# Split-product attention for two heads at a time, run between the projection tiles of the other heads

## The reference

```python
q, k, v, f_logit, c_b, c_c, c_in, gate_a, gate_c = split_cols(u @ w_in)
log_f = log_sigmoid(f_logit + b_forget)
F = cumsum(log_f, axis=1)
s = einsum('bqhd,bkhd->bhqk', q, k) * 64 ** -0.5
s = s + F_q[..., None] - F_k[:, :, None, :]
s = where(k_pos <= q_pos, s, -inf)
y_attn = einsum('bhqk,bkhd->bqhd', softmax(s), v)
y_conv = c_b * short_conv(c_c * c_in, conv_w)
mixed = (sigmoid(gate_a) * (y_attn @ w_attn_branch) + sigmoid(gate_c) * (y_conv @ w_conv_branch)) @ w_out
```

## Time and profile before

| | |
|---|---|
| median of 3 runs | 2390.04 us |
| the profiled execution, as a run | 2395.49 us |
| its span | 2393.8 us |
| TensorE busy | 2243.4 us, 94% |
| VectorE busy | 1019.3 us, 43% |
| ScalarE busy | 712.7 us, 30% |
| POOL busy | 620.3 us, 26% |
| granted TensorE clock, mean | 0.91 |

### The profile page before, as it was taken

How to read it: one execution, slowest core, us unless ns; L and a number is a source line. 1 busy time by engine, 2 the same in 40 slices (tenths; PEclk the granted TensorE clock), 3 DMA queues, 4 the chain that set the end, 5 groups by cost and what they waited for, 6 DMA issues and landing times.

```text
span 2393.8 us, 29247 instructions
## 1 busy us (share of the span) xinstructions
PE 2243.4 (94%) x11946; PEld 1857.1 (78%) x11946; DVE 1019.3 (43%) x1621; ACT 712.7 (30%) x909; POOL 620.3 (26%) x147
## 2 busy tenths in 40 slices
PE   6999985999997999979999997999999988999997
PEld 6698874888766666669999997887578776888886
DVE  4699764423327566542322235302442324332224
ACT  2422232322225545431111123323342223122121
POOL 0334300234310000024433331231004332434430
PEclk6999985799998999989999996898569997999998
DMA  8455400132214999732222221121003321232210
GB/s 245 135 179 183 137 18 1 36 106 88 70 36 141 337 341 342 279 106 89 88 90 92 98 88 36 54 88 54 0 1 107 105 71 53 89 104 88 94 64 36
DMA packets 176219, 261.30 MB, mean 109 GB/s; under 512 B 13209, under 2 KB 141898, under 8 KB 176126
## 3 DMA queue, kind: packets, MB, share of 16 engines
q1 hardware_dynamic: 175550, 258.96, 32.2%
q10 hardware_dynamic: 576, 1.05, 0.1%
HBM read 257.88 MB, written 2.11 MB: 109 GB/s over the span
## 4 chain that ended last, share of the span: by engine, by line
PE 82%; DVE 14%; issue 1%; ACT 1%; DMA 1%; SPq 0%; DVEq 0%; ACTq 0%
PE PS L690 56%; PE PS L1109 6%; PE PS L1131 4%; PE PS L924 3%; DVE macc L1760 2%; PE PS L1223 2%; PE PS L746 1%; DVE Hf L1731 1%; DVE sc L1875 1%; DVE max L1874 1%; PE PS L915 1%; DVE macc L1758 1%; DVE Hf L1712 1%; PE PS L890 1%; PE PS L840 1%
## 5 line engine op out<-in xcount | busy, mean ns | idle before, releaser
L652 POOL TENSOR_TENSOR w_lo<-w_raw,w_hi 128x2048 fp32r<-128x2048 f32 x133 | 617.9, 4648 | 1689.6 <-ACT w_hi L1313 1689.6
L690 PE MATMUL PS<-HH,w_hi 128*128 128x512 f32 (+1 forms) x1936 | 598.2, 347 | 25.2 <-DVE HL L1705 25.2
L690 PE MATMUL PS<-HL,w_hi 128*128 128x512 f32 (+1 forms) x1936 | 598.7, 347 | 0.0
L690 PE MATMUL PS<-HH,w_lo 128*128 128x512 f32 (+1 forms) x1936 | 596.3, 346 | 0.0
L1313 ACT ACTIVATE w_hi<-w_raw 128x2048 fp32r<-128x2048 f32 x133 | 254.3, 1913 | 534.0 <-PE PS L690 491.9
L690 PEld LDWEIGHTS PS<-HH,w_hi 128*128 128x128 f32 x1936 | 339.2, 191 | 74.8 <-issue 28.0
L690 PEld LDWEIGHTS PS<-HL,w_hi 128*128 128x128 f32 x1936 | 338.5, 190 | 45.5
L690 PEld LDWEIGHTS PS<-HH,w_lo 128*128 128x128 f32 x1936 | 338.1, 190 | 45.0
L2278 DVE TENSOR_TENSOR actf<-PS,sg 128x528 f32<-128x528 f32 (+1 forms) x44 | 30.8, 700 | 421.0 <-PE PS L690 421.0
L2289 DVE TENSOR_TENSOR yacc<-yacc,PS 128x528 f32<-128x528 f32 (+1 forms) x176 | 122.4, 695 | 105.7 <-PE PS L690 105.7
L2171 DVE TENSOR_TENSOR m_lo<-m_raw,m_hi 128x2048 fp32r<-128x2048 f32 x56 | 128.1, 2292 | 77.3 <-ACT m_hi L1520 76.8
(11 more groups left out here) (356 smaller groups left out, 2878.8 us busy)
## 6 DMA issues: line engine op xcount, KB each, us to landing
w_raw<-in_w_in SPq DMA_DIRECT2D x49, 1024.0 KB, 5.1
w_raw<-in_w_ffn_in SPq DMA_DIRECT2D x44, 1024.0 KB, 4.9
m_raw<-in_w_exp_gate SPq DMA_DIRECT2D x56, 512.0 KB, 4.3
m_raw<-in_w_exp_up SPq DMA_DIRECT2D x56, 512.0 KB, 5.5
m_raw<-in_w_exp_down SPq DMA_DIRECT2D x56, 512.0 KB, 4.8
w_raw<-in_w_ffn_out SPq DMA_DIRECT2D x22, 1024.0 KB, 4.8
mod_raw<-in_w_mod SPq DMA_DIRECT2D x20, 1024.0 KB, 5.0
w_raw<-in_w_out SPq DMA_DIRECT2D x8, 1024.0 KB, 5.0
```

Source lines behind the costliest of these rows:

```text
L652: pool.tensor_tensor(w_lo[:, s, :], w_raw[:, s, :], w_hi[:, s, :].bitcast(F32), ALU.subtract).then_inc(split, 1)
L690: ins = mm(o, l, r, **k)
```

## The change

1. The ring of weights has two arrays instead of three: `w_lo` lies where `w_raw` lies. So the load of chunk c waits for TensorE's start of chunk c−2 (`begun`), not for the split of c−3. The slot of expert chunk 3 moves to the freed room at the other end.
2. The spread of the forget sums is gone. VectorE writes the sums' hi and lo parts to `FS` and a selecting matrix `selF`, and a fourth product adds them to the logits; a fifth, of the identity and the mask `outR`, adds the mask.
3. Q, K, V and the probabilities are split into hi (ScalarE) and lo (VectorE), and logits and values are made of three products each. A step handles two heads (partitions 0 to 63 and 64 to 127) and one query tile; the values of two query tiles are made at once. There are 16 steps.
4. The chunks of `P2` come in the order K, Q, V of heads 0 to 3, then K, Q, V of heads 4 to 7. Behind each of the 9 tiles of the latter one attention step (`fox_step`) is issued; the others follow after.

```diff
-        w_raw = at("w_raw", B, [RING, CH]); B += RING * CH * 4
+        w_raw = at("w_raw", B, [RING, CH])
+        w_lo = at("w_lo", B, [RING, CH], F32R); B += RING * CH * 4
         w_hi = at("w_hi", B, [RING, CH], F32R); B += RING * CH * 4
-        w_lo = at("w_lo", B, [RING, CH], F32R); B += RING * CH * 4
...
-        for x, off in enumerate([BASE + 16384 * q for q in range(4)] + [A0 + 49152, A0 + 16384]):
+        for x, off in enumerate([BASE + 16384 * q for q in range(3)] + [A0 + 81920, A0 + 49152, A0 + 16384]):
...
-              ("fm", K2), ("fm", K2 + 256), ("fm", Q2), ("fm", Q2 + 256), ("tm", V2), ("tm", V2 + 256)]
-        FORGET_AT, SPREAD_AT = 2, 4
+              ("fm", K2), ("fm", Q2), ("tm", V2), ("fm", K2 + 256), ("fm", Q2 + 256), ("tm", V2 + 256)]
+        KQV = [c0 for _, c0 in P2[6:]]
+        FOX_FROM = 9
+        FORGET_AT = 2
+        FOX = [(m, i) for m in range(4) for i in range(NTOK)]
...
                 if c >= RING:
-                    sp.wait_ge(split, c - RING + 1 + more)
+                    sp.wait_ge(begun, c - RING + 2 + more)
...
+            def fox_logits(m, i):
...
+                cols = [slice(0, min(512, n_all))] + ([slice(512, n_all)] if n_all > 512 else [])
+                for n, (q_, k_) in enumerate(((qh, kh), (qh, kl), (ql, kh), (None, None))):
+                    for cs in cols:
+                        for e in range(2):
+                            hp = slice(64 * e, 64 * e + 64)
+                            if n < 3:
+                                mm(outs[e][:, cs], q_[hp, m, rows], k_[hp, m, cs], start=n == 0, stop=False, skip_group_check=True)
+                            else:
+                                h = 2 * m + e
+                                mm(outs[e][:, cs], selF[hp, h:h + 1].to_broadcast([64, P]), FS[hp, cs], start=False, stop=False,
+                                   skip_group_check=True)
+                d0 = META + P * i
...
+                        ins = mm(outs[e][:, c0:cs.stop], identR[:, :], outR[:, c0 - d0:cs.stop - d0], start=False, stop=True,
+                                 skip_group_check=True)
...
+            def fox_transposes(x):
...
+                pe.wait_ge(pn2_ready, x + 1)
+                for part in range(1 if i < NTOK - 1 else 2):
...
+                            nc.tensor.transpose(PS[:, s, b, P * j:P * j + P], src[:, META + P * j:META + P * j + P], ident[:, :])
...
+            def fox_values(x):
...
+                W.wait_released(tgroup[x])
+                s = W.claim()
+                for e in range(2):
...
+                    for j in [4] + list(range(2 * hf_ + 2)):
+                        q0 = P if j == 2 * hf_ + 1 else 0
...
+                        for n, (l, r) in enumerate(((vh, ph_), (vl, ph_), (vh, pl_))):
+                            ins = mm(o[:, q0:256], l[kp, j, vs], r, start=j == 4 and n == 0, stop=j == 2 * hf_ + 1 and n == 2,
+                                     skip_group_check=True)
...
+            def fox_step():
+                n = at_step["n"]
+                at_step["n"] += 1
+                if n == 8:
+                    for g in range(1, 5):
+                        W.wait_released(W.g - g)
+                if n < len(FOX):
+                    fox_logits(*FOX[n])
+                if 0 <= n - 2 < len(FOX):
+                    fox_transposes(n - 2)
+                if 0 <= n - 4 < len(FOX) and FOX[n - 4][1] % 2 == 1:
+                    fox_values(n - 4)
...
-                if n_p == SPREAD_AT:
+                after = None
+                if n_p >= FOX_FROM:
+                    after = fox_step
...
+            while at_step["n"] < len(FOX) + 4:
+                fox_step()
```

More of the change, by code:

```diff
@@ L718, in fm_chunk @@
                     W.made(ins)
+                    if after is not None:
+                        after()
                 cur["h"] = None
@@ L722, in h_operands, with tm_chunk @@
                 return (lambda k: HH[:, k, t0_:t0_ + T]), (lambda k: HL[:, k, t0_:t0_ + T])
-            def tm_chunk(tiles):
+            def tm_chunk(tiles, after=None):
                 s_w = begin_chunk()
@@ new lines, in fox_transposes @@
+            def fox_transposes(x):
+                m, i = FOX[x]
+                pe.wait_ge(pn2_ready, x + 1)
+                for part in range(1 if i < NTOK - 1 else 2):
+                    s = W.claim()
+                    for e in range(2) if i < NTOK - 1 else (part,):
+                        src = pr2[:, x % 3, e, :]
+                        for j in range(i + 1):
+                            b = e if i < NTOK - 1 else 0
+                            nc.tensor.transpose(PS[:, s, b, P * j:P * j + P], src[:, META + P * j:META + P * j + P], ident[:, :])
+                        b, c0 = (e, P * (i + 1)) if i < NTOK - 1 else (1, 0)
+                        ins = nc.tensor.transpose(PS[0:META, s, b, c0:c0 + P], src[:, 0:META], ident[:, :])
+                    W.made(ins)
+                tgroup[x] = W.g - 1
@@ new lines, in _ @@
+            for x, c0 in enumerate(KQV):
+                next_hi()
+                for t in range(2 if x % 3 < 2 else 5):
+                    s = W.arrive()
+                    W.skip(1)
+                    m = 2 * (x // 3) + t
+                    if x % 3 == 0:
+                        ins = af(sv(kh[:, m, :], TALL), ps(s, TALL), ACT.Copy)
+                    elif x % 3 == 1:
+                        ins = af(qh[:, m, :], ps(s), ACT.Copy)
+                    else:
+                        n, vc = P if t < 4 else META, c0 - V2
+                        ins = af(vh[0:n, t, vc:vc + 256], PS[0:n, s, 0, 0:256], ACT.Copy)
+                    ins.then_inc(kqv_hi, 1)
+                    if x >= 3:
+                        fox_step()
@@ L2326, in _ @@
             W.skip(1)
+            L.mark(ts(FS[:, :], ones[:, 0:1].to_broadcast([P, TALL]), 0.0, None, ALU.mult))
+            L.mark(ts(selF[:, :], ones[:, 0:8], 0.0, None, ALU.mult))
+            L.mark(v_.tensor_copy(identR[:, :], ident[:, :]))
+            L.mark(v_.tensor_copy(outR[:, :], outside[:, :]))
+            L.wait()
+            for b in range(4):
+                L.mark(v_.tensor_copy(selF[32 * b:32 * b + 8, :], ident[32 * b:32 * b + 8, 32 * b:32 * b + 8]))
             dve.wait_ge(gla_act, 2 + seq + 1 + 1)
@@ new lines, in _, with fox_step @@
+            t_at = {}
+            at_step = {"n": 0}
+            def fox_step():
+                n = at_step["n"]
+                at_step["n"] += 1
+                if 0 <= n - 3 < len(FOX):
+                    fox_lo(n - 3, t_at[n - 3])
+                if n < len(FOX):
+                    fox_max(n)
+                if 0 <= n - 1 < len(FOX):
+                    fox_scale(n - 1)
+                if 0 <= n - 2 < len(FOX):
+                    t_at[n - 2] = W.g
+                    W.skip(1 if FOX[n - 2][1] < NTOK - 1 else 2)
+                if 0 <= n - 4 < len(FOX) and FOX[n - 4][1] % 2 == 1:
+                    W.skip(1)
```

252 lines of the change are left out of this document (174 added, 78 removed).

## The result

| | before | after |
|---|---|---|
| median | 2390.45 us (2389.11 to 2393.1, 4 runs) | 2413.02 us (2408.12 to 2418.24, 4 runs) |
| ratio of the two, 95% interval | | 1.0093 (1.0068 to 1.0119) |
| span of the profiled run | 2393.8 us | 2406.3 us |
| granted clock, mean | 0.91 | 0.92 |

The changed kernel is 22.6 us slower; the forecast was 2403 for the median and 2407 for the span.

A forecast was written before the change was run, and what follows sets the result against it. TensorE was taken as the bound: attention's fp32 work at half clock, with VectorE near-full in the first projection. Terms −14.4 − 130.4 + 90 + 66 + 2 = +13.2 us gave span 2407, median 2403, range 2366 to 2438.

The forecast's parts named there:

- The turns: First projection: w_mod loads queue behind w_in loads, so 14 turns take 16.4 us instead of 11.7, +66 us.
- TensorE's product of macc and the next start: + 0.5: Last step of a first-projection turn, taking it from B + 15.9 to B + 16.4, B being TensorE's chunk start.
- The spread: Forget sums before the attention: removing TensorE's eight spreading products and the clock loss behind them saves 14.4 us.
- The merges: Ends of the two merges: VectorE's last sums meet POOL's split, +1 us each, +2 in all.
- The feed-forward: Feed-forward stages: the changed weight loads were priced at nothing there; stalls would make the prediction fall.
- The attention: Second attention: 130.4 us replaced by 90, from 38 us in the interleaved part and 52 in the lone steps.
- I take the latter: Attention's small split products: 128 columns priced at the fp32 0.21 us, not the other bound of 0.11.
- Rival 1: First projection: the wait on loads costs little, turns of 12.8 us, +15 instead of +66: 2352; chance 0.13.
- Rival 2: Lone attention steps at half clock: their 43 us become 83 with fewer stalls, +35: 2438; chance 0.22.
- Rival 3: Attention at its lower bound of 69 us, small products at 0.11 and pipeline dense: 2382; chance 0.17.
- small products at 0.11, no drain: Conditions given for the attention's lower bound of 69 us, against the 90 forecast.
- Rival 4: Attention: the pairs of heads don't overlap, +0.5 to 1 us a step over 16 steps, +10: 2413; chance 0.1.

The follow-up runs named there:

- the wait alone: Kernel before with one line changed, a weight load waiting for TensorE's start of chunk c−2 instead of POOL's split of chunk c−3: 2473.3 us, ratio 1.033.
- the split moved: Kernel after, with POOL's split in the first projection waiting until VectorE has made the same turn's macc, load order unchanged: 2361.9 us, ratio 0.986.
- the run with the mask between the heads: Kernel after with w_mod loads ahead of w_in loads, one head's logits after the other and the mask's 128-row product between them: 2367.9 us.
- the 128-row run: The 2367.9 us kernel (heads one after the other, mask between), with logits over all 128 rows, summing both heads, a wrong formula: 2329.9 us.
- early loads: Kernel after, with the w_mod load of turn n+1 issued ahead of the w_in load of turn n: 2332.8 us, and 2330.3 on another chip.
- the 16 paired steps in a row: Kernel after with w_mod loads ahead of w_in loads, all attention steps behind the last chunk instead of nine between its tiles: 2334.4 us.

## Why the prediction was right, and where it was not

- **The turns.** The mechanism was right in each step: 8.0 us for the tile (8.3 forecast), the first product 4.06 (4 forecast) and its end at the split's end, the rest as worked out. The turn came out 16.8, not 16.4, so +71 and not +66. The missing 0.4 is in the step "TensorE's product of macc and the next start: + 0.5": the four products took 1.01 us in this turn instead of 0.50, since the clock was at its lower level from 124.2 to 131.0, behind TensorE's gap of 4.2 us. I had allowed for a lower clock in the next chunk, which has slack, and not for the one piece of TensorE's work that stands in the chain. The two chunks behind the turns, at 0.91 instead of 1.00, cost 2.5 us more, which I had not priced either. Three runs show the cause: the wait alone (+81), the loads exchanged (all of it back), the split moved (51 back).
- **The spread.** −14.3 us, −14.4 forecast. Nothing took its place. The sum of the windows shows it; no run took it alone.
- **The merges.** +2 forecast, since VectorE's last sums would meet POOL's split. The two stages took 249.9 and 184.1 us, against 249.9 and 183.6: +0.5. The feed-forward, priced at nothing, took nothing (388.5 us for its first part, against 388.9).
- **The attention: 82.0 us, 90 forecast.** TensorE's work was overpriced. The term that failed is "I take the latter", the fp32 price of 0.21 us for a small split product, and with it the lower of its two bounds, 0.11. At full clock 128 columns take 0.06 us and 256 take 0.12, each with its weight load:

```profile
1786.23 0.28 PE L1284 MATMUL PS<-PT0h,vl 128*64 128x256 f32 x1
1786.35 0.28 PE L1284 MATMUL PS<-PT0l,vh 128*64 128x256 f32 x1
1786.46 0.22 PE L1284 MATMUL PS<-PT0h,vh 128*64 128x128 f32 x1
1786.52 0.22 PE L1284 MATMUL PS<-PT0h,vl 128*64 128x128 f32 x1
```

  Read the distance of the starts, not the lengths. The 0.11 us of a load with a single column, which I took for a floor, comes from an fp32 operand, which I take for its reason; no run parts it. In the steps at full clock the logits of the four query tiles took 0.87, 0.98, 1.21 and 1.9 us (1.7, 1.25, 1.5 and 2.2 forecast), the values 2.3 and 3.7 with 3.4 us of transposes: 14.4 us for a pair of heads, 57 for all, where I had 72. So stalls and half clock make 25 us, not 18. The interleaved part took 72.4 (75 forecast) and the lone one 46.8 (52). That two heads side by side count as one was right; that it would be worth 10 us was too much for the overlap (2 us by the stretches, nothing by the medians) and too little for what it does to the clock.
- **Rival 1** (turn of 12.8) came about in the run with POOL's split moved: 2361.9, where the prediction had 2352 and the expectation 2359. That it "decides by 0.8 us" holds: the split began 0.7 us before the product.
- **Rival 2** (lone steps at half clock) came only for 14 of 47 us, 0.85 there, and the run with the mask between the heads shows what would have made it come: the reason that I gave against it, that the 64-row logits now come in pairs, is what kept it away. The rule of the Trainium skill weighed there (TensorE: Matmul & The Clock Gate, Part 4, that full rate is not reached for transpose-mode products) does not decide here: the lone steps of the 128-row run held 1.00 with all their transposes in.
- **Rival 3** (the attention at 69 us) did not come, though one of its two conditions did: small products cost even less than its 0.11 us. The other, a dense pipeline, did not. Its price was also wrongly added: at 0.11 instead of 0.21 us, 48 products of 128 columns and the logits of the shortest query tile save 7 us, and the drain 3, so "small products at 0.11, no drain" is 80 us and not 69; even without the 9 us of stalls in the lone steps it is 71. The measured 82.0 lies nearer to this 80 than to the forecast's 90. (The 2.2 us for the logits of the longest tile is 2.1 by its own terms.)
- **Rival 4**, that the pairs don't overlap, did not come, and its price of 10 was too low: the run that parts the heads costs 35, by the clock.
- **Not foreseen: +2.7 us at the start.** TensorE's half clock there lasted 51.2 us instead of 44.4. Over all profiled runs it lasted from 44.4 to 64.9 us, and it differs between two runs of the same kernel: 47.8 and 44.4 with early loads, where the w_mod load of 84.63 in before stands at 86.04 and 84.55. So I take it for chance between runs.

The sum, +13.2, came within 1 us of the +12.5 of the span, by luck: −8 in the attention and +8 in the turns and the chunks behind them cancel, and so do +2.7 at the start and −3.1 in the rest (−1.1 measured, where the forecast had the +2 of the merges). The median lies 10 us above the forecast since I put it below the profiled run, as it was before (by 5.0 in the end); of after's runs the profiled one is the lowest, 4.9 below the median.

## To carry to other kernels

When a wait in a DMA queue is exchanged, write down everything behind it in that queue with the time at which each is needed; an unrelated load that landed 8 us into its turn cost more here (74 us) than all the saved arithmetic gave (63). Then ask under what the delayed work now falls: VectorE's products lost more to POOL's split than to the late tile, and the load issued ahead of the wait cured both. And for TensorE count rows as well as time: logits on 64 rows with nothing beside them were paid at half clock here, so try to put the other half of the rows to work even where the overlap by itself brings little. It is no guarantee: two stretches at half clock with all rows in use stand above.

## What the runs showed of the hardware

- **Row count and clock.** TensorE busy 72.4 of 75.1 us, on logits of 64 rows one head at a time: granted clock 0.59. The same products on 128 rows: 1.00 (45.8 us). In pairs on both halves: 0.96 (45.1 us). The Trainium skill (TensorE: Matmul & The Clock Gate, Part 1) puts the half rate down to idle gaps; here the stretch at half rate had fewer gaps (2.7 us) than the one at full rate (4.7 us), so gaps alone do not tell the two apart. Nor does the row count in every case: the old attention with its logits on 128 rows ran 47.8 us at 0.50, and the 16 paired steps in a row ran 30.7 us at it.
- **Order of products.** A product on rows 64 to 127 started at 1782.27, before one on rows 0 to 63 at 1782.61 that stands ahead of it in the queue. The same page, Part 3, says that products start strictly in order and only weight loads are pulled ahead; these rows differ from it. With a product on all 128 rows between them, the heads stayed in order (1705.83, then 1706.35).
- **VectorE and POOL.** A product of VectorE of 0.34 us whose operands all lie in SBUF took 4.06 when it began 0.7 us after POOL's split, ending 0.15 after it. A scaling of two columns took 2.51 us in the same way, while the reduction just before it, which reads PSUM under the same split (POOL from 1695.03 to 1699.64), took the 0.98 us that it takes without one:

```profile
1696.15 0.98 DVE L2505 TENSOR_REDUCE nmax<-PS 128x2 f32<-128x800 f32 x1
1697.16 2.51 DVE L2512 TENSOR_SCALAR nmax<-nmax 128x2 f32<-128x2 f32 x1
```

  The Trainium skill (SBUF — State Buffer, SBUF: two separate sides) describes the port pair that the two engines share as an exclusive lock held for the whole instruction; the trace agrees.
- **Small split products.** 128 columns at 0.06 us and 256 at 0.12 at full clock, weight load included.
